# Odd layer's block inverses: 128x128 transposes in place of products for the transposed side, and blocks stored by token tile

## What is computed

```python
def rwkv7_scan(r, logw, k, v, kk, a, s0):
    def step(s, inp):
        r_t, lw_t, k_t, v_t, kk_t, a_t = inp
        sa = jnp.einsum('bhvk,bhk->bhv', s, -kk_t)
        s = (s * jnp.exp(lw_t)[:, :, None, :] + sa[..., None] * (kk_t * a_t)[:, :, None, :]
             + v_t[..., None] * k_t[:, :, None, :])
        return s, jnp.einsum('bhvk,bhk->bhv', s, r_t)
...
y_f, sf_f = rwkv7_scan(rh, log_decay(0), kh, vh, kk, ah, s0_f)
y_b, sf_b = rwkv7_scan(flip(rh), flip(log_decay(1)), flip(kh), flip(vh), flip(kk), flip(ah), s0_b)
```

## Time and profile before

| | us |
|---|---|
| median of three runs | 1579.1 |
| lowest and highest | 1577.63, 1582.22 |
| profiled execution | 1576.2 |
| its span, first to last instruction | 1574.3 |
| TensorE busy | 1487.2 (94%) |
| VectorE busy | 545.6 (35%) |
| ScalarE busy | 296.3 (19%) |
| mean granted clock | 0.984 |

### The profile page before, as it was taken

How to read it: one execution, slowest core, us unless ns; L and a number is a source line. 1 busy time by engine, 2 the same in 40 slices (tenths; PEclk the granted TensorE clock), 3 DMA queues, 4 the chain that set the end, 5 groups by cost and what they waited for, 6 DMA issues and landing times.

```text
span 1574.3 us, 62507 instructions
## 1 busy us (share of the span) xinstructions
PE 1487.2 (94%) x28005; PEld 1323.4 (84%) x28005; DVE 545.6 (35%) x1410; ACT 296.3 (19%) x817; POOL 16.4 (1%) x32
## 2 busy tenths in 40 slices
PE   5999888999998999999887999999999999999995
PEld 3888477999546787888866999999999999999995
DVE  1463435666636344666843301010101011010102
ACT  2112423010102432444324101010101010010101
POOL 0100000000000000000000000000000000000000
PEclk9999998999998999999998999999999999999998
DMA  9722676444448144000132799999999999999993
GB/s 391 292 82 100 250 300 270 161 174 181 182 167 314 40 162 150 6 8 8 33 151 81 300 417 379 416 386 418 384 412 409 387 419 380 418 376 417 376 418 131
DMA packets 72895, 407.07 MB, mean 259 GB/s; under 512 B 10514, under 2 KB 10948, under 8 KB 35908
## 3 DMA queue, kind: packets, MB, share of 16 engines
q1 hardware_dynamic: 68176, 398.92, 64.0%
q0 software_dynamic: 1184, 3.41, 0.7%
q10 hardware_dynamic: 3412, 2.93, 0.6%
HBM read 403.31 MB, written 1.92 MB: 257 GB/s over the span
## 4 chain that ended last, share of the span: by engine, by line
PE 37%; PEld 10%; DVE 1%; ACT 1%; issue 1%; PEldq 0%; DVEq 0%; POOL 0%; ACTq 0%
PE bank L1466 20%; PE bank L1486 10%; PEld bank L1466 7%; PEld bank L1486 3%; PE bank L644 2%; PE bank L1448 1%; PE bank L1432 1%; PE bank L1442 0%; PEld bank L1432 0%; PE bank L709 0%; PE bank L1267 0%; PEld bank L1448 0%; DVE w L2036 0%; DVE w L2675 0%; PE bank L1290 0%
## 5 line engine op out<-in xcount | busy, mean ns | idle before, releaser
L1466 PE MATMUL bank<-w,ring 128*64 128x86 f32 x11264 | 452.6, 237 | 1.1 <-ACT w L1959 0.6
L1466 PEld LDWEIGHTS bank<-w,ring 128*64 128x64 f32 x11264 | 432.4, 136 | 9.7 <-issue 8.8
L1486 PE MATMUL bank<-w,ring 128*64 128x86 f32 x5632 | 238.7, 237 | 0.0
L2860 DVE TENSOR_TENSOR w<-w,bank 128x86 f32<-128x86 f32 x176 | 43.1, 245 | 549.0 <-PE bank L1466 541.6
L1486 PEld LDWEIGHTS bank<-w,ring 128*64 128x64 f32 x5632 | 220.8, 137 | 0.0
L1971 ACT ACTIVATE w<-bank 128x86 f32<-128x86 f32 x176 | 42.8, 243 | 572.4 <-PE bank L1466 572.4
L641 PE MATMUL bank<-w,ring 128*128 128x256 f32 x256 | 59.1, 394 | 4.3 <-DVE w L2454 3.7
L641 PEld LDWEIGHTS bank<-w,ring 128*128 128x128 f32 x256 | 50.5, 198 | 13.0 <-DVE w L2454 4.0
L644 PE MATMUL bank<-ring,w 128*128 128x256 f32 x256 | 56.0, 380 | 1.9 <-DVE w L2036 1.9
L644 PEld LDWEIGHTS bank<-ring,w 128*128 128x128 f32 x256 | 48.4, 190 | 8.8 <-DVE w L2036 2.3
L667 PE MATMUL bank<-ring,ct 128*32 128x256 f32 x768 | 47.0, 396 | 2.4 <-ACT ct L1569 2.1
(11 more groups left out here) (437 smaller groups left out, 1795.9 us busy)
## 6 DMA issues: line engine op xcount, KB each, us to landing
ring<-in_moe_gu SPq DMA_DIRECT2D x176, 1024.0 KB, 8.5
ring<-in_moe_w_down SPq DMA_DIRECT2D x176, 512.0 KB, 8.6
ring<-in_ada_w SPq DMA_DIRECT2D x48, 1024.0 KB, 5.0
ring<-in_ev_w_in SPq DMA_DIRECT2D x11, 1024.0 KB, 26.6
ring<-in_ffn_w_gate SPq DMA_DIRECT2D x11, 1024.0 KB, 7.9
ring<-in_ffn_w_up SPq DMA_DIRECT2D x11, 1024.0 KB, 5.2
ring<-in_ffn_w_down SPq DMA_DIRECT2D x11, 1024.0 KB, 6.4
ring<-in_ev_w_out SPq DMA_DIRECT2D x4, 1024.0 KB, 11.0
```

The costliest lines, as they stand in the source:

```text
L1466: ins = [mm(b[hp, 0:CAP], w[:, k, hp], XG[:, k, :], start=k == 0, stop=k == KC - 1, skip_group_check=True) for hp in HALVES]
L1486: ins = [mm(bank[4 + c // 4][hp, (c % 4) * CAP:(c % 4 + 1) * CAP], w[:, c * P + hp.start:c * P + hp.stop], HIDU[:, t % 2, :], start=t == 0 ...
L2860: v.tensor_tensor(HIDU[:, t % 2, :], SILU[:, t % 2, :], bank[2 + t % 2][:, 0:CAP], ALU.mult).then_inc(sem("hid"), 1)
```

## The change

At levels 1 to 4 the products that make the new P are gone. `turned_x(i, lv)` transposes the merged X instead, four times 128x128 with the identity: two 64x64 blocks of X (the two token groups) stand one below the other in partitions on one side, and side by side on the other. ScalarE copies the wanted columns from the bank to IP (`take_turned`). Level 5 keeps its products (`last_p`, `last_wider`). `turned_start` becomes four such transposes.

For this the blocks are stored by token tile: an IP block lies in the partitions of its token group (`HALVES[j // 2]`), with head, and token half h, along the columns; Z, the right sides (`GS`) and the results in the banks follow. `z` now writes output half `HALVES[j // 2]` from input half `hp` into `bank[h]`; `new_x` reads input half `HALVES[j // 2]` and writes output half `hp` into `bank[2 + st]`. `right_side` and `solve` use banks 6 and 7 together, `last_states` bank 1 (bank 7 in the last pass). The eight banks are one tensor, so that an instruction can read two. `wider` has four instructions a level in place of two, `start_inverse` eight half as wide in place of four, `take_right` one in place of two.

The order changes: on TensorE `t4(i, 2)` moves to the end of the pass before, `turned_keys` to level 2, `t4(i+1, 0)` and `t4(i+1, 1)` a place forward, `right_side` (from pass 1 on) between `new_x(i, 4)` and `z(i, 5)`. On ScalarE `decays` is split over two places and `take_keys` moves forward. On VectorE `masked(i, 2)` opens the pass and `start_states` moves ahead of `wider(i, 4)`. `new_x(i, lv)` waits for Z's copies and for the turned copies of the level before.

```diff
-        bank = [ctx.enter_context(nc.psum_tensor(f"bank{i}", [P, 512], F32)) for i in range(8)]
+        banks = ctx.enter_context(nc.psum_tensor("banks", [P, 4096], F32))
+        bank = [banks[:, i * 512:(i + 1) * 512] for i in range(8)]
...
-        IP = [tiles4(HTf[:, 512 * k:512 * k + 512]) for k in range(2)]
-        IX, IZ = tiles4(HTf[:, 1024:1536]), tiles4(HTf[:, 1536:2048])
-        GS = tiles4(GBf[:, 0:512])
+        IP = [HTf[:, 512 * k:512 * k + 512].rearrange("p (d a h n) -> p d a h n", d=2, a=2, h=2) for k in range(2)]
+        IX, IZ = HTf[:, 1024:1536].rearrange("p (d a b n) -> p d a b n", d=2, a=2, b=2), tiles4(HTf[:, 1536:2048])
+        GS = GBf[:, 0:512].rearrange("p (r d a n) -> p r d a n", r=2, d=2, a=2)
...
-                    pe.wait_ge(sem("zc"), 10 * i - 1 + d)
-                for j in range(4):
-                    for hp in HALVES:
-                        at = home(d, hp)
-                        ins = mm(bank[2 + d][hp, j * DH:(j + 1) * DH], IP[i % 2][at, d, j, :], ID2[at, :], start=True, stop=True)
-                        if j == 3:
-                            ins.then_inc(sem("z"), 1)
+                    pe.wait_ge(sem("zc"), 18 * i)
+                for a in range(2):
+                    at = (2 * d + a) * P
+                    ins = tr(bank[3][:, at:at + P], IP[i % 2][:, d, a, :, :].rearrange("p h n -> p (h n)"), ident)
+                ins.then_inc(sem("z"), 2)
 
             def z(i, lv):
 
                 if lv == 1:
                     pe.wait_ge(sem("x0"), 2 * i + 2)
                     pe.wait_ge(sem("m4"), 4 * i + 2)
-                    if i:
-                        pe.wait_ge(sem("inv"), 10 * i)
+                    if i >= 2:
+                        pe.wait_ge(sem("so"), i - 1)
                 else:
                     pe.wait_ge(sem("ix"), 8 * i + 2 * (lv - 1))
                 for j in range(4):
+                    to = HALVES[j // 2]
                     for d in range(2):
-                        for hp in HALVES:
-                            ins = mm(z_bank(lv, d)[home(d, hp), j * DH:(j + 1) * DH], M4[i % 2][0][hp, j, 0, queries(d, hp), :],
-                                     IX[hp, d, j, :],
+                        at = (j % 2) * 256 + d * DH
+                        for h, hp in enumerate(HALVES):
+                            ins = mm(bank[h][to, at:at + DH], M4[i % 2][0][hp, j, 0, queries(d, hp), :],
+                                     IX[hp, d, j % 2, j // 2, :],
                                      start=True, stop=True)
                             if j == 3:
                                 ins.then_inc(sem("z"), 1)
 
-            def xp(i, lv):
-                pe.wait_ge(sem("zc"), 10 * i + 2 * lv)
-                if lv > 1:
-                    pe.wait_ge(sem("inv"), 10 * i + 2 * (lv - 1))
-                if lv < 5:
-                    for j in range(4):
-                        for d in range(2):
-                            for hp in HALVES:
-                                at = home(d, hp)
-                                ins = mm(z_bank(lv + 1, d)[hp, j * DH:(j + 1) * DH], IP[i % 2][at, d, j, :], IZ[at, d, j, :],
+            def new_x(i, lv):
+
+                if lv == 1:
+                    pe.wait_ge(sem("zc"), 18 * i + 2)
+                    if i:
+                        pe.wait_ge(sem("inv"), 2 * i)
+                else:
+                    pe.wait_ge(sem("zc"), 18 * i + 4 * lv - 2)
+                for j in range(4):
+                    st, a = j // 2, j % 2
+                    for d in range(2):
+                        at = a * 256 + d * DH
+                        for h, hp in enumerate(HALVES):
+                            ins = mm(bank[2 + st][hp, at:at + DH], IP[i % 2][HALVES[st], d, a, h, :], IZ[HALVES[st], d, 2 * h + a, :],
+                                     start=True, stop=True)
+                            if j == 3:
+                                ins.then_inc(sem("nx"), 1)
+
+            def turned_x(i, lv):
+
+                pe.wait_ge(sem("ix"), 8 * i + 2 * lv)
+                for d in range(2):
+                    for a in range(2):
+                        at = (2 * d + a) * P
+                        ins = tr(bank[2][:, at:at + P], IX[:, d, a, :, :].rearrange("p b n -> p (b n)"), ident)
+                    ins.then_inc(sem("np"), 1)
+
+            def last_p(i):
+
+                pe.wait_ge(sem("zc"), 18 * i + 18)
+                for d in range(2):
+                    for a in range(2):
+                        for h in range(2):
+                            at = (4 * d + 2 * a + h) * DH
+                            for to in HALVES:
+                                ins = mm(bank[2][to, at:at + DH], IZ[to, d, 2 * h + a, :], IP[i % 2][to, d, a, h, :],
                                          start=True, stop=True)
-                                if j == 3:
-                                    ins.then_inc(sem("nx"), 1)
-                for d in range(2):
-                    for j in range(4):
-                        for hp in HALVES:
-                            ins = mm(z_bank(lv, 0)[hp, (4 * d + j) * DH:(4 * d + j + 1) * DH], IZ[hp, d, j, :], IP[i % 2][hp, d, j, :],
-                                     start=True, stop=True)
-                            if d == 1 and j == 3:
-                                ins.then_inc(sem("np"), 1)
+                                if (d, a, h) == (1, 1, 1):
+                                    ins.then_inc(sem("np"), 1)
...
-                    col = {d: 0, 1 - d: 256}
-                    for n, hp in enumerate(HALVES):
-                        mm(bank[6][hp, col[n] + 2 * DH:col[n] + 4 * DH], NQ[i % 3][:, d, 1, 0, hp], S0P[:, d, :],
-                           start=d == 0, stop=True, skip_group_check=True)
+                    hp = second(d)
+                    for part, q in enumerate((first(d), second(d))):
+                        mm(bank[6 + d][HALVES[1], part * P:part * P + P], NQ[i % 3][:, d, 1, 0, q], S0P[:, d, :],
+                           start=part == 0, stop=True, skip_group_check=True)
                     for j in range(4):
-                        hp = second(d)
-                        ins = mm(bank[6][hp, 256 + j * DH:256 + (j + 1) * DH], M4[i % 2][1][:, j, 0, queries(d, hp), :],
-                                 v_of(i, j // 2, j % 2), start=False, stop=True, skip_group_check=True)
-                        if d == 1 and j == 3:
-                            ins.then_inc(sem("g"), 1)
+                        st, a = j // 2, j % 2
+                        mm(bank[6 + d][HALVES[st], P + a * DH:P + (a + 1) * DH], M4[i % 2][1][:, j, 0, queries(d, hp), :],
+                           v_of(i, st, a), start=j == 0, stop=True, skip_group_check=True)
                 for j in range(4):
+                    st, a = j // 2, j % 2
                     for d in range(2):
                         hp = first(d)
-                        ins = mm(bank[6][hp, j * DH:(j + 1) * DH], M4[i % 2][1][hp, j, 0, queries(d, hp), :],
-                                 v_of(i, j // 2, j % 2)[hp], start=False, stop=True, skip_group_check=True)
-                        if d == 1 and j == 3:
+                        ins = mm(bank[6 + d][HALVES[st], a * DH:(a + 1) * DH], M4[i % 2][1][hp, j, 0, queries(d, hp), :],
+                                 v_of(i, st, a)[hp], start=False, stop=True, skip_group_check=True)
+                        if j == 3:
                             ins.then_inc(sem("g"), 1)
...
             def solve(i, part):
 
-                pe.wait_ge(sem("gs"), 4 * i + 2 * part + 2)
+                pe.wait_ge(sem("gs"), 2 * i + part + 1)
                 if part == 0:
-                    pe.wait_ge(sem("inv"), 10 * i + 10)
-                    if i:
-                        pe.wait_ge(sem("so"), i)
-                    else:
-                        pe.wait_ge(sem("mod"), 12)
+                    pe.wait_ge(sem("inv"), 2 * i + 2)
                 for j in range(4):
+                    st, a = j // 2, j % 2
+                    at = HALVES[st]
                     for d in range(2):
                         hp = second(d) if part else first(d)
-                        at = HALVES[part]
-                        ins = mm(bank[7][hp, (4 + j) * DH:(5 + j) * DH], IP[i % 2][at, d, j, :], GS[at, d, j, :],
-                                 start=True, stop=True)
+                        to = 256 + d * P + a * DH
+                        ins = mm(bank[6 + st][hp, to:to + DH], IP[i % 2][at, d, a, hp.start // DH, :], GS[at, part, d, a, :],
+                                 start=False, stop=True, skip_group_check=True)
...
                 else:
-                    t4(i, 2)
-                xp(i, 1)
+                    t4(i, 3)
+                new_x(i, 1)
                 if i:
                     carry(i - 1)
                 z(i, 2)
+                turned_x(i, 1)
                 if i == 0:
                     half_v(3, 1)
                 else:
```

(61 more changed lines are left out.)

106 lines of the change are left out of this document (54 added, 52 removed).

## The result

The changed kernel takes 1601.6 us (median of 4, 1598.3 to 1603.0) against 1580.2 for the kernel before (median of 4, the three shown ahead of the prediction and one beside the changed kernel): 21.3 us or 1.33% slower, ratio 1.0133 with a 95% interval of 1.011 to 1.0156. The forecast was 1598. The profiled execution took 1602.2 us with a span of 1600.4, which is 26.1 longer than that of before; the profiled execution of before (1576.2) lay 4 us under its median, so the medians differ by less than the two profiles.

A forecast was written before the change was run, and what follows sets the result against it. The loop was taken as bound by TensorE's pace of starting small products. Six middle passes at 2.1 us, +4.5 for the first, +3 for the last, less 1 for "issue", gave +19: 1598 us, range 1577 to 1610.

The forecast's parts named there:

- (a): Middle pass, levels 1 to 4: four blocks of P products become transposes, 0.88 to 0.72 us each, saving 0.64.
- (b): `turned_start` on TensorE becomes four transposes: 0.93 against 0.72 us, saving 0.21 a pass.
- (c): `z` and X products use two tiles at a time under the new storage: 9 x 0.24 = 2.16 us added a pass.
- (e): Without P as cover, `z(i,2)` waits 0.8 us and `z(i,3)` 0.5 for `wider`; `z(i,4)` and `z(i,5)` are covered.
- (f): VectorE opens the pass with `masked(i,2)` behind longer `start_inverse` and `sums`; `t4(i,3)` waits about 0.7 us.
- "issue" stalls: TensorE idle time in the loop with no releaser in the profile, 6 us, to shrink by about 1 us.
- Rival 1: PSUM banks, not tiles, set TensorE's pace, so (c) costs nothing: +2 to +7 us, 1583 us; chance 0.16.
- Rival 2: Faster than before: rival 1's pace, transposes at 0.45 us, waits covered: -9, 1570 us; chance 0.13.
- Rival 3: Slower still: new blocks run like P (0.88), transposes and `wider` at 0.85: +36, 1615 us; chance 0.05.

The follow-up runs named there:

- e4: The kernel before with only the loops of `z` and the X products turned, d outermost, so two tiles are used at a time; 1585.55 us.
- e1: The changed kernel with one VectorE edit, `masked(i+1,0)` behind `wider(i,3)` instead of ahead of it; 1589.91 us.
- e2: The changed kernel with `z` and `new_x` loops reordered so all four tiles follow in turn, same banks; 1586.43 us.
- e3: The changed kernel with both four-tile order in `z` and `new_x` and `masked(i+1,0)` behind `wider(i,3)`; 1574.18 us.
- e5: The kernel of e3 with `masked(i+1,2)` moved to right behind `last_wider(i)`, ahead of `sums`; 1572.25 us.
- e7: The changed kernel with only `masked(i+1,2)` moved to right behind `last_wider(i)`, ahead of `sums`; 1600.24 us.
- e6: The kernel of e5 with every transpose of `turned_x` issued twice into the same place; 1582.92 us.

## Why the prediction held, and where it did not

The total is right (1598 against 1601.6) and so are the sign and one of the two main causes, but several terms are wrong and cancel in part; that the total comes so near is partly luck. Against the profiled execution from which it was worked out, the forecast was +19 and the profiles differ by 26. The loop was forecast at 212 us and takes 217.3. A middle pass was forecast at 23.8, and those without a fall of the clock take 25.0 to 25.3, or 25.8 in pass 6. The base of 21.7 was one pass; the six of the kernel before average 22.8, with 4.5 of the 6.7 us of "issue" in them.

**(a), (b), transposes.** Estimated at 0.72 a block, bounds 0.45 to 0.85; measured 0.49 (ahead of `turned_keys`, which is 128x128 too), 0.58 to 0.59 (ahead of `t4`) and 0.73 (ahead of `last_states`). So they are cheaper than taken, by some 0.12 on average over the five of a pass (`turned_start`, 0.59, among them). The rule of the Trainium skill that was weighed in (a), "TensorEngine Tiling (Array Packing)", Key Properties, by which a change of mode drains TensorE, agrees with the trace: the block of 0.49 is the one with no change of mode behind it. The sign of the term was right. By starts, the four blocks of a middle pass save 4 x 0.88 - 2.4 = 1.1 us where 0.64 was forecast, or 9 us over eight such passes where 5.1; the 14.8 us above are merged times, which overlap with their neighbours.

**(c), the order of the tiles.** This term carried the forecast: 9 x 0.24 x 8 = 17.3 us. The blocks measure 0.98 and 0.93 (forecast 0.95), and undoing the order gives 15.2 us. The size is right, but it holds here for a reason that the prediction did not give: full-width work follows five of the nine blocks of a pass. e4 shows that the same order costs some 0.1 a block where mostly 64x64 products follow.

**(e), the chains. This is the step that failed, though the total held.** "`z(i,4)` and `z(i,5)` are covered by `outputs` (2.55) and `right_side` (1.8)" looked only at what TensorE issues meanwhile. The diff moves `masked(i+1,0)` ahead of `wider(i,3)`, and its wait on the reader of its buffer, `outputs(i-1)` itself, was not followed. The cover and what it was to cover thus wait for each other in turn: 1.75 us six times, 10.5 us, all of it missing from the sum. e1 shows it. The other two waits of the step were forecast at 0.8 and 0.5 and measure 0.56 and 0.51. `wider` was estimated at 0.60 and 0.90 and takes 0.61 and 0.72.

**(f).** `t4(i,3)` forecast to wait 0.7, measured 0.54; `start_inverse` 2.6, measured 2.50. In pass 7 about 3, measured 2.7.

**The "issue" stalls.** Forecast to shrink by 1 us; all 6.7 went. This is the term that hid the miss in (e), together with pass 0: +4.5 forecast, +1.9 measured. Its four `z` wait 2.9 us (3.7 forecast), but the kernel before had 2.5 us of idle time there and not the 1.1 that was taken. The middle passes show the miss: +3.0 us each on average, where 2.1 was forecast, and +3.3 to +3.6 from the pass of 21.7 that was taken as the base to those without a fall of the clock.

**The clock.** Not in the sum at all. Two middle passes are some 1.7 us longer than their neighbours where it falls, about 3.4 us, and pass 7 has 6 us at half clock.

**The rivals.** Rival 1 (banks) needed `z` at 0.69 in the changed kernel, where it is 0.98, and e2 brings 0.69 with the same banks; it is out. Rival 2 named the point from which it decides, `z` under 0.55 and transposes under 0.5. With four tiles in turn `z` has 0.62 to the next block and transposes 0.5 to 0.7, and the kernel comes out faster once `wider` is free too (e3). Rival 3 had the middle pass at 4.2 us more; it was 3.0 on average.

## What to carry to other kernels

Price a block of small matmuls by the time until the next block can start, which depends on whether the tiles used last are those that the next one needs; alternate all the tiles of the array inside a block, above all where full-width work follows. When an instruction is moved up on an in-order engine, follow each of its waits back to the engine that it serves: if it waits for work that stands just ahead of the critical consumer, everything queued behind it inherits that wait. A wait removed on a chain of several can be worth less than its length, so count on it in full only when the next wait has been looked at (e5 and e7 gave 2.0 and 1.4 us, both near what the runs can tell from nothing, where 5 to 6 were expected).

## What was not expected of the hardware

- Blocks of the same 32 MATMULs take 0.47 us to their last start with four tiles in turn and 0.75 (0.97 less 0.22) with two. A block of 64x64 products for other tiles begins 0.57 to 0.59 us behind the start of the slow one, while a 128-wide one has to wait 0.86 to 0.90.
- The changed kernel, e2 and e7 have a wait of 1.75 to 1.78 us at `z(i,4)` in each of their six middle passes; behind it the granted clock fell to 0.50 in 2, 1 and 2 of the six. The other eight kernels do not have that wait, and there is not one fall in their 48 middle passes. What decides it each time was not found. Longer waits do not settle it either: behind 2.47 us at `z(7,2)` of e5 the clock fell, behind 2.68 us at the same place of e6 it did not, nor behind an "issue" wait of 2.25 us in the kernel before.
- The stalls that the profile puts under "issue", 6.7 us in the loop before, were absent from the loop of the changed kernel, and 2.0 us in e4, with an unchanged number of instructions. The number of instructions does not tell them.
